# A gated convolution layer in split fp32: the output projection by a round of seven products for eight, attention behind the products' work

## The reference

```
h    = rms_norm(x, pre_norm)
proj = h @ w_in                      # 3*1024 conv, 1536 gate, 512 memory queries
b, c, u = conv part;  z = c * u
mix  = b * (conv_w[0]*z[t-2] + conv_w[1]*z[t-1] + conv_w[2]*z[t])
kv   = rms_norm(mem, mem_norm) @ w_mem_kv            # 4 heads of 128
mem_o = softmax(mq k^T * 128**-0.5) v                # 4096 tokens x 256 keys, per head
y    = (concat([mix, mem_o]) * silu(gate)) @ w_out   # 1536 -> 1024
out  = x + rms_norm(y, post_norm)
```

## Time and profile before

| | |
|---|---|
| time, median of 3 runs | 2373.96 us (2372.81 to 2376.64) |
| the profiled execution | 2373.23 us, span 2371.5 us |
| mean granted clock of TensorE | 0.975 |
| PE busy / weight loads | 2237.3 us (94%) / 1851.6 us (78%) |
| DVE, ACT, POOL busy | 1110.3, 711.0, 60.9 us |
| matmuls of the input rounds | 3 x 2240, 0.39 us each as modelled |
| matmuls of the output groups | 3 x 768 |

### The profile page before, as it was taken

The page is one execution under the profiler, slowest core; times in us unless marked ns, Lnnn a source line. Parts: engine busy times, 40 slices in busy tenths (PEclk is TensorE's granted clock), DMA queues, the critical chain, the costliest instruction groups (busy, mean ns, idle before and its releaser), DMA issues.

```text
span 2371.5 us, 26241 instructions
## 1 busy us (share of the span) xinstructions
PE 2237.3 (94%) x10074; PEld 1851.6 (78%) x10074; DVE 1110.3 (47%) x1735; ACT 711.0 (30%) x1257; POOL 60.9 (3%) x108
## 2 busy tenths in 40 slices
PE   3899999999999999999999999997489999999997
PEld 2687878788888888888888888776378888888886
DVE  8577776713552243444351353231544444444531
ACT  4333433411211131221131121111444444444430
POOL 0000000000000000000000000000000000000000
PEclk9899999999999999999999999999599999999999
DMA  4686666777566677666577655547323333333321
GB/s 153 236 310 242 250 251 244 265 258 249 194 205 213 219 246 254 227 207 213 193 242 256 208 196 182 207 166 246 122 80 107 107 107 107 107 107 107 107 76 53
DMA packets 158235, 445.82 MB, mean 188 GB/s; under 512 B 13952, under 2 KB 46752, under 8 KB 155936
## 3 DMA queue, kind: packets, MB, share of 16 engines
q1 hardware_dynamic: 139984, 376.49, 46.3%
q0 software_dynamic: 18128, 67.66, 8.4%
HBM read 320.36 MB, written 123.73 MB: 187 GB/s over the span
## 4 chain that ended last, share of the span: by engine, by line
PE 85%; DVE 8%; DMA 3%; issue 2%; ACT 1%; SPq 0%; DVEq 0%; POOL 0%; ACTq 0%; POOLq 0%
PE banks L1162 28%; PE banks L1163 28%; PE banks L1164 28%; DVE hop_lo L811 2%; DMA slots<-w_split 2%; PE banks L1282 1%; DVE x_in L789 1%; DVE x_in L807 1%; DVE slots L841 1%; DMA q_raw<-q_kept 1%; DMA x_in<-in_x_t 0%; DVE wo_lo L1055 0%; DVE st_w L835 0%; DVE acc L784 0%; DMA conv_raw<-g_kept 0%
## 5 line engine op out<-in xcount | busy, mean ns | idle before, releaser
L1162 PE MATMUL banks<-hop_hi,slots 128*128 128x512 f32 x2240 | 882.7, 394 | 50.3 <-DVE hop_lo L811 22.3
L1163 PE MATMUL banks<-hop_lo,slots 128*128 128x512 f32 x2240 | 877.1, 392 | 0.0
L1164 PE MATMUL banks<-hop_hi,slots 128*128 128x512 f32 x2240 | 876.7, 391 | 0.0
L1162 PEld LDWEIGHTS banks<-hop_hi,slots 128*128 128x128 f32 x2240 | 424.0, 189 | 147.5 <-issue 43.7
L1164 PEld LDWEIGHTS banks<-hop_hi,slots 128*128 128x128 f32 x2240 | 423.8, 189 | 89.3
L1163 PEld LDWEIGHTS banks<-hop_lo,slots 128*128 128x128 f32 x2240 | 424.0, 189 | 88.7 <-issue 1.4
L1162 PE MATMUL banks<-wo_hi,gc_hi 128*128 128x512 f32 x512 | 202.6, 396 | 0.0
L1163 PE MATMUL banks<-wo_lo,gc_hi 128*128 128x512 f32 x512 | 199.9, 391 | 0.0
L1164 PE MATMUL banks<-wo_hi,gc_lo 128*128 128x512 f32 x512 | 199.7, 390 | 0.0
L886 DVE TENSOR_TENSOR u<-banks,u 128x512 f32<-128x512 f32 x56 | 38.7, 690 | 297.4 <-PE banks L1164 297.4
L579 ACT ACTIVATE s<-banks 128x512 f32<-128x512 f32 x80 | 47.8, 598 | 416.7 <-PE banks L1164 416.7
(11 more groups left out here) (137 smaller groups left out, 2344.7 us busy)
## 6 DMA issues: line engine op xcount, KB each, us to landing
slots<-w_split SPq DMA_DIRECT2D x420, 512.0 KB, 3.4
w_split<-slots SPq DMA_DIRECT2D x140, 512.0 KB, 2.9
raws<-in_w_in SPq DMA_DIRECT2D x80, 256.0 KB, 3.9
x_in<-in_x_t SPq DMA_DIRECT2D x16, 1024.0 KB, 6.9
g_kept<-mix POOLq DMA_DIRECT2D x16, 1024.0 KB, 6.6
x_res<-in_x POOLq DMA_DIRECT2D x32, 512.0 KB, 5.0
conv_raw<-g_kept SPq DMA_DIRECT2D x32, 512.0 KB, 4.6
out_x<-x_res POOLq DMA_DIRECT2D x32, 512.0 KB, 3.4
```

The costliest lines, as they stand in the source:

```text
L1162: nc.tensor.matmul(dst, a, c, start=first, stop=False, skip_group_check=True)
L1163: nc.tensor.matmul(dst, a, d, start=False, stop=False, skip_group_check=True)
L1164: return nc.tensor.matmul(dst, b, c, start=False, stop=last, skip_group_check=True)
```

## The change

- The convolution part of the output projection becomes a fifth round (OUT) of the seven-product form. `w_conv`, the 1,024 conv rows of `w_out`, takes the place of the tokens (`load_x` at pairs 16 and 17 of the last macro, two 1 MB loads at each) and becomes `hop_hi`, `hop_lo`. The gated conv results take the place of the weights: 16 pairs of 256 tokens, 112 units, built from four chunks of 256 KB a pair as in macro 0 (`ahead`: four units ahead, also in the last four steps of macro 3). Each pair's sums go to DRAM (`y_kept`).
- The memory part (4 inner blocks, 24 matmuls per 128 tokens) is done after the round, in 32 steps: its token operand is one unit per step, its weights are split into `hop` (`operand_hi/lo(OUT + 1, ...)`), DVE adds `y_kept` to PSUM (`sum_up`), and norm and residual are made in passes of 1,024 columns (`finish`). The gated memory results go through DRAM (`mem_kept`). The mean square is now one pass on ACT.
- Attention goes along with the round, three steps a head from step 6 on (FIRST_SCORE). On PE each attention operation stands behind a product; on ACT and DVE it stands behind that step's copy, add and `ahead`.
- The memory keys and values are made 4 pairs sooner (KV_AFTER), their norm 24 steps sooner; they are kept in DRAM (`kv_kept`) while `w_conv` is in their place, and come back at step 2.
- `g_kept` is laid out by 128 tokens and is written by two DMAs a group with rows of 512 bytes. The splits of `w_out`, `wo_split`, `conv_split`, `mem_split` and the ramp go.

The step loops of the new round:

```
# PE
+for step in range(OUT_UNITS):
+    pair, r = divmod(step, PRODUCTS)
+    multiply(ALL_PAIRS + pair, r)
+    n, phase = divmod(step - FIRST_SCORE, 3)
+    if phase == 0 and 0 <= n < HEADS:
+        score(n)
+    if phase == 1 and 0 <= n - 1 < HEADS:
+        weigh(n - 1)
+    if phase == 2 and 0 <= n < HEADS:
+        turn(n)
# ACT
+    evacuate(ALL_PAIRS + pair, r)
+    ahead(OUT, step)
+    if step == R5:
+        operand_hi(OUT, R4)
+    if pair == OUT_PAIRS - 1 and r in (R6, R3):
+        operand_hi(OUT + 1, R1 if r == R6 else R5)
+    n, phase = divmod(step - FIRST_SCORE, 3)
+    if phase == 1 and 0 <= n + 1 < HEADS:
+        query(n + 1)
+    if phase == 1 and 0 <= n < HEADS:
+        soften(n)
+    if phase == 0 and 0 <= n - 1 < HEADS:
+        turned(n - 1)
# DVE
+    if r in (R3, R7, R2):
+        add(ALL_PAIRS + pair, r)
...
+    ahead(OUT, step)
+    if pair == OUT_PAIRS - 1 and r in (R7, R4):
+        operand_lo(OUT + 1, R1 if r == R7 else R5)
+    n, phase = divmod(step - FIRST_SCORE, 3)
+    if phase == 2:
+        if 0 <= n - 1 < HEADS:
+            gate(n - 1)
+        if 0 <= n < HEADS:
+            soften(n)
+        if 0 <= n + 1 < HEADS:
+            query(n + 1)
+    if phase == 0 and 0 <= n - 1 < HEADS:
+        turned(n - 1)
+    if phase == 1 and 0 <= n < HEADS:
+        row_maxima(n)
```

What holds a unit back, and the memory part:

```
 def build_hi(u, src):                    # ACT, unchanged
     slot = u % SLOTS
     if u >= SLOTS:
         act.wait_ge(unit_done, u - SLOTS + 1)
# SP, in the round
+    if phase == 0 and 0 < n + 1 < HEADS and step >= FIRST_SCORE:
+        load_q(n + 1)
+    if phase == 0 and 0 <= n - 1 and n < HEADS:
+        load_m(n)                        # waits for mem_gated of head n-1
# SP, last macro
+    if i in OUT_X_AFTER and m + 1 == MACROS:     # {16: (0, 1), 17: (2, 3)}
+        sp.wait_ge(kv_kept_dma, 16 * 4)
+        for n in OUT_X_AFTER[i]:
+            load_x(n, OUT)
# DVE, memory part
+for n in range(NT * SUB):
+    sum_up(n)
+    if n + SLOTS < NT * SUB:
+        mem_unit_lo(n + SLOTS)
+    if n:
+        finish(n - 1)
# POOL, memory part
 for n in range(NT * SUB):
-    pool.wait_ge(y_final, 2 * n + 2)
+    pool.wait_ge(y_final, n + 1)
     pool.dma_start(out[n * P:(n + 1) * P, :], x_res[:, n % 2, :]).then_inc(out_dma[n % 2], 16)
     if n + 2 < NT * SUB:
         load_residual(n + 2)
```

More of the change, by code:

```diff
@@ L64, with kind_of, built_pair, trunk @@
         LOADS[_u] = sum(1 for v in LOADS if v % SLOTS == _u % SLOTS) + 1
+def kind_of(p):
+    return KINDS[p % PAIRS] if p < ALL_PAIRS else "y"
 def count(kinds, p):
-    return sum(KINDS[n % PAIRS] in kinds for n in range(p))
-def trunk(nc, x, x_t, mem, in_gains, post_g, conv, w_in, w_kv, w_out, out):
+    return sum(kind_of(n) in kinds for n in range(p))
+def built_pair(p):
+    return p if p < PAIRS else PAIRS + p - ALL_PAIRS
+def trunk(nc, x, x_t, mem, in_gains, post_g, conv, w_in, w_kv, w_conv, w_mem, out):
     f32 = mybir.dt.float32
@@ L431, in _, with load_y @@
[L431 to L453, removed]
+            def load_y(n):
+                if n >= YP:
+                    sp.wait_ge(y_final, n - YP + 1)
+                sp.wait_ge(y_kept_dma, 16 * (n // 2 + 1))
+                sp.dma_start(y_sum[:, n % YP, :], y_kept[n // 2][:, n % 2 * D:(n % 2 + 1) * D]).then_inc(y_dma[n % YP], 16)
@@ L647, in _ @@
                         operand_hi(0, {R5: R7, R6: R2, R7: R4}[r])
-                    if m == 0 and step + SLOTS < UNITS0:
-                        unit_hi(step + SLOTS)
-                    if m + 1 < MACROS and i == PAIRS - 1 and r != R6:
+                    ahead(m, step)
+                    if i == PAIRS - 1 and r != R6:
                         operand_hi(m + 1, {R1: R1, R5: R5, R3: R6, R7: R3, R2: R7, R4: R2}[r])
@@ L960, in _ @@
                 norm(0, k)
-            build(0)
+            build(0, 0)
             inverse(1)
@@ L1002, in _ @@
                         token_sum(0, 3)
-                    if m == 0:
-                        build(step + SLOTS)
-                    if m + 1 < MACROS and i == PAIRS - 1:
+                    ahead(m, step)
+                    if i == PAIRS - 1:
                         if r in (R5, R6, R7, R2, R4):
@@ L1114, in finish @@
                 dve.wait_ge(yrs_done, n + 1)
-                for half in range(2):
-                    y = psum[:, (2 * n + half) % 4, :]
-                    nc.vector.scalar_tensor_tensor(out=y, in0=y, scalar=yrs[:, one],
-                                                   in1=post_gain[:, half * HALF:(half + 1) * HALF],
-                                                   op0=ALU.mult, op1=ALU.mult).then_inc(y_scaled, 1)
-                dve.wait_ge(x_res_dma[n % 2], 16 * (n // 2 + 1))
-                for half in range(2):
-                    y = psum[:, (2 * n + half) % 4, :]
-                    row = x_res[:, n % 2, half * HALF:(half + 1) * HALF]
-                    dve.wait_ge(y_scaled, 2 * n + half + 1)
-                    nc.vector.tensor_tensor(row, y, row, ALU.add).then_inc(y_final, 1)
@@ new lines, in finish @@
+                nc.vector.scalar_tensor_tensor(out=y, in0=y, scalar=yrs[:, one], in1=post_gain[:],
+                                               op0=ALU.mult, op1=ALU.mult).then_inc(y_scaled, 1)
+                dve.wait_ge(x_res_dma[n % 2], 16 * (n // 2 + 1))
+                dve.wait_ge(y_scaled, n + 1)
+                nc.vector.tensor_tensor(row, y, row, ALU.add).then_inc(y_final, 1)
+            dve.wait_ge(post_dma, 16)
+            for n in range(NT * SUB):
+                sum_up(n)
+                if n + SLOTS < NT * SUB:
+                    mem_unit_lo(n + SLOTS)
+                if n:
+                    finish(n - 1)
@@ L1158, in _ @@
+            finish(NT * SUB - 1)
         @block.tensor
@@ L1311, in _ @@
-            pe.wait_ge(kv_lo_done, KV_BLOCKS)
-            for step in range(-9, 8 * NT):
-                if step % 2:
-                    if 0 <= (step + 7) // 2 < NT * MH:
-                        weigh((step + 7) // 2)
-                    if 0 <= (step + 9) // 2 < NT * MH:
-                        score((step + 9) // 2)
-                elif 0 <= (step + 8) // 2 < NT * MH:
-                    turn((step + 8) // 2)
-                if step >= 0:
-                    group(step)
+            for step in range(OUT_UNITS):
+                pair, r = divmod(step, PRODUCTS)
+                multiply(ALL_PAIRS + pair, r)
+                n, phase = divmod(step - FIRST_SCORE, 3)
+                if phase == 0 and 0 <= n < HEADS:
+                    score(n)
[3 more added lines that the diff above has]
+                    turn(n)
```

546 lines of the change are left out of this document (296 added, 250 removed).

## The result

Over rounds that alternated with the kernel before, the changed kernel took 2583.36 us (median; 2578.02 to 2587.46), the kernel before 2375.25: ratio 1.0876, 95% interval 1.0852 to 1.0901. The prediction said 2479, with a range to 2545, and the time lies 38 us beyond it. The direction was right and the amount too small by half: the span of the profiled executions grew by 212 us (2371.5 to 2583.7) where 106 were forecast.

What follows compares the result with a forecast made beforehand. PE's instruction stream was taken as the bound. Start 1656 + round 614.6 + first wait 1.6 + memory part 188.8 + end 16.6 = 2477.6 of span; with 1.7 around it 2479 us, range 2415 to 2545.

Steps and rivals of the forecast that it cites:

- Round's start: End of the last input round: from 1644.9, with 6 us for new loads and 5 for the turn, to 1656.
- the 5 that were allowed: Turn of the round: DVE's 4 sums and 4 splits beside seven 2,048-column operations stop PE; bounds 2 and 8.
- The turn's wait: New round: PE idles before each head's transposes for the scaled probabilities, mean 4.67 us, 149 over 32 heads.
- The first rival: At turn(n): probabilities ready when product 2 ends, so no wait and no low clock; 2285 us, chance 0.06.
- The clock: New round: PE falls to its lower clock after the turn's waits, 1.4 us a head, 45 in all.
- the rows of 4.91 and 2.05 us: Earlier profile rows: after 4.91 us idle PE was at its lower level, after 2.05 it was not.
- the bound of 2.1: Upper bound per head on time lost to PE's low clock: ten matmuls at 0.43 us after 4.91 us idle.
- the case that every head pays: New round: the clock falls in every head, costing 67 us instead of 45; time 2501.
- The other handovers are covered: New round: pt of step 0 takes some 3.3 us beside score and product, 4.2, so no further wait.
- The memory part: 32 steps after the round at 5.9 us, 188.8 in all; lower bound PE's 5.45, upper 7.1.
- The loop that the prediction priced: Memory part, two x_res buffers: issue, store landing, load landing, add; 10.3 us for two steps, 5.15 each.
- The third rival: Memory part: the residual's loop binds at 7.0 a step, 2514; 2537 with the clock falling in every head; chance 0.17.

Runs made afterwards that it cites:

- experiment 1: The changed kernel with DVE's attention work ahead of its add and unit building, ACT's left behind: 2432.62 us, ratio 1.0248.
- experiment 2: The changed kernel with attention first on ACT and DVE, and DVE's gate and scalings one step sooner: 2404.84 us, ratio 1.0128.
- experiment 3: The changed kernel with 18 useless matmuls of 512 columns ahead of each turn, so PE does not stand idle: 2520.7 us, ratio 1.0617.
- experiment 6: The kernel of experiment 4 (eight residual buffers), but POOL waits for each store to land before it goes on: 2577.1 us, ratio 1.0860.
- experiment 7: The changed kernel, still two residual buffers, with SP issuing the residual loads and POOL stores alone, without waiting for them: 2522.89 us, ratio 1.0626.
- experiment 5: The changed kernel without the residual's loads after the first two; POOL still waits for each store to land: 2500.93 us, ratio 1.0539.
- after: The changed kernel itself, as measured against the kernel before: 2583.36 us, ratio 1.0876.
- experiment 4: The changed kernel with eight residual buffers instead of two, loaded four steps ahead: 2501.91 us, ratio 1.0536.

## Why the prediction was right and wrong

**Round's start, right** (1653.2 for 1656). The loads took 4.82 of the 6. The turn of the round took the 5 that were allowed, but not all before the start: 1.03 before the last input product, and 3.96 four products into the new round. There PE waited for ACT's copy of a bank, which stood behind a high part of the new operand, and that behind DVE's difference of 2,048 columns:

```profile
1665.66 1.91 ACT L687 ACTIVATE hop_hi<-x_in 128x2048 fp32r<-128x2048 f32 x1 [5.71 <-DVE x_in L900]
```

Some 2 us of the start are in neither wait and were not taken apart.

**The turn's wait, right.** Each link stood where it was put, 4.4 to 5.0 a head (5.5 in the first), 150.8 in all for 149.4. Its reason, two in-order engines in which attention stands behind the unit work, is shown by experiments 1 and 2, which changed only the order of the same instructions and took back 96 and 122 us of it. The first rival's argument, "DVE and ACT are half idle", was none for this order: shares of busy time say nothing of who stands behind whom.

**The clock, mechanism right, size wrong.** The prediction took two falls in three, 1.4 a head, a hedge between the rows of 4.91 and 2.05 us. It fell in every head, and also behind the two start-up waits. By experiment 3 a fall costs 1.94 us, so the bound of 2.1 that the earlier trace rows gave was good and the discount to two in three was the error: 62 us in the turns and about 3 behind the start-up waits, for 45. The prediction's own sum for the case that every head pays was 67. The 12 us that remain of the 77.3 are not the low level, since the round of experiment 3 has them at clock 1.00; about half are the sum's prices, a little low: a turn and the product behind it take 3.69 at full clock, where the sum has 0.79 and 2.73.

**One start-up wait, missed.** 4.27 us for DVE's q_lo of the first head: ACT had waited for that head's query to land. The prediction priced the handovers in the steady state alone ("The other handovers are covered").

**The memory part, the step that failed.** 66.8 us of the 106. The prediction put 5.9 us a step on it, and it took 7.93. The loop that the prediction priced, "The output row of a step must leave before the next residual comes", has two landings for two steps. POOL's program has a tighter one: `load_residual(n + 2)`, which waits for store n, stands ahead of store n + 1 in POOL's order, so each step holds a whole landing, 7.2, and an issue of 0.53, 7.7 in sum against 7.93 measured. Experiment 6 has this wait without the two buffers and stays at 2577; experiment 7 has the two buffers without the wait and comes to 6.08 a step, 0.2 from the price of 5.9. That price was 5.15 from its rows and the rest an allowance, and the landings in the loop were 7.1 and 3.6 where it had 3.7 and 5.0, so the nearness is partly luck. The third rival, that the residual's loop binds, named the place and part of the size (2514; 2537 with the clock), but by longer landings in the priced loop; that loop alone gives the 6.08. The Trainium skill, DMA: Bandwidth & Descriptors, "Latency and other measured facts", lets HBM's access grow by up to 1.8 us under load; by that the priced loop came to 14 us for two steps, which is 7.0 a step and 2514; the 2517 of the prediction is a slip. The median landing of the store grew by 3.8 here and that of the load by 1.4, together 5.2 where the page's figure gives 3.6, and 2.2 of the store's growth went with the load beside it (experiment 5). How much of this is HBM and how much the company of other transfers, no run here shows.

Not settled: whether a store lands late because of what is ahead of it on its queue or because of what is in flight at all, and why waits of one length between 1.8 and 3.4 us lower the clock at one time and not at another.

## What to carry to other kernels

Write out, for each in-order engine, what stands between an instruction and the one before it: POOL's wait for its own store just issued made eight buffers worth no more than two, and neither the DMA share (0.69) nor the bytes showed it. Price an idle PE of over 4 us with the slow work behind it, here 1.9 us for a wait of 4.7. Where a change puts new work onto engines that are half idle, the order within each engine decides its sign: the same products cost 8.8% or saved 3.5%.

## What the hardware showed that was not expected

- In the output stage of four kernels (after, experiments 1 to 3) PE was at its low level behind all 48 waits of 3.9 us and more, and behind none of 0.8 to 1.8. Between 1.8 and 3.4 us, most of them in the memory part, it went both ways: in after it stood at 1.00 behind waits of 2.39 and 2.59 and fell behind 3.32.
- The same 512 KB store landed in 3.4 us in the kernel before, and in the memory part in 5.0 without the residual's loads (experiment 5) and 7.2 with one issued 0.53 us before it (after), at 242 and 221 GB/s. In experiment 7, with the loads on SP, it took about 7 when issued within 0.3 us of another load and about 4.6 otherwise. What was issued beside it told more than the mean traffic.
- 336 GB/s at a DMA share of 0.95 with landings of 7.1 and 8.1 us left PE without a wait in the memory part (experiment 4). Landings that long did no harm there, since the issue was early enough.
